# Reordered layer norm halves, masks on VectorE, GLA norm between gates, and cross attention over two sets of PSUM banks, in a streaming encoder step

## The reference

```python
x = layer_norm(ALPHA * x + 0.5 * swiglu(x, lw['w_ffn1_in'], lw['w_ffn1_out']), g[0], b[0])
mix, new_pool, ckv, kr, new_gla = token_mixing(x, pos0, pool_hist, gla_state, ckv_past, kr_past, lw)
x = layer_norm(ALPHA * x + mix, g[1], b[1])
x = layer_norm(ALPHA * x + memory_attend(x, mem_k, mem_v, lw['mem_w_q'], lw['mem_w_o']), g[2], b[2])
x = layer_norm(ALPHA * x + 0.5 * swiglu(x, lw['w_ffn2_in'], lw['w_ffn2_out']), g[3], b[3])
```

## Time and profile before

| | us |
|---|---|
| median of 3 runs | 3211.24 |
| lowest, highest | 3206.44, 3216.93 |
| profiled execution, whole | 3221.17 |
| its span in the trace | 3219.4 |

### The profile page before, as it was taken

One profiled execution on the slowest core, in us unless ns is written; L12 is line 12 of the kernel. 1 busy time (PEld: TensorE's weight loads), 2 busy tenths in 40 slices (PEclk: granted clock), 3 DMA queues, 4 the chain that ended last, 5 costly groups with the idle time before them and its releaser, 6 DMA issues.

```text
span 3219.4 us, 54799 instructions
## 1 busy us (share of the span) xinstructions
PE 3012.8 (94%) x22470; PEld 2860.8 (89%) x22470; DVE 1082.6 (34%) x1818; ACT 911.7 (28%) x1392; POOL 1092.7 (34%) x454
## 2 busy tenths in 40 slices
PE   7999999999899799999999999899998987999995
PEld 7999987689898589999999999867998975899995
DVE  3111255543335352112331112555334253511123
ACT  2222242322334232222232222432223341422223
POOL 3444322033271224434334333311333611344331
PEclk9999999999999899999999999989999998999998
DMA  3222222022252012222222222211222510222222
GB/s 134 91 85 86 92 68 68 15 73 79 75 194 66 27 53 92 88 88 86 80 83 85 91 86 79 83 40 40 67 80 88 188 53 27 71 87 85 91 87 81
DMA packets 74438, 259.83 MB, mean 81 GB/s; under 512 B 10704, under 2 KB 13648, under 8 KB 72848
## 3 DMA queue, kind: packets, MB, share of 16 engines
q1 hardware_dynamic: 65520, 238.58, 23.1%
q10 hardware_dynamic: 8736, 18.64, 1.6%
HBM read 249.32 MB, written 7.87 MB: 80 GB/s over the span
## 4 chain that ended last, share of the span: by engine, by line
PE 85%; DVE 6%; ACT 3%; issue 2%; DVEq 1%; ACTq 1%; DMA 0%; SPq 0%
PE PS L286 84%; ACT Y L836 2%; DVE XL L1193 1%; DVE Y L1193 1%; DVE CP L1713 1%; DVEq L1264 1%; ACT XH L836 1%; ACTq L1169 0%; DVE SC L1476 0%; PE PS L784 0%; PE PS L555 0%; ACT LNT L836 0%; DMA WR<-in_w 0%; DVE PT L1501 0%; DVE SC L1702 0%
## 5 line engine op out<-in xcount | busy, mean ns | idle before, releaser
L276 POOL TENSOR_TENSOR WL<-WR,WH 128x1024 fp32r<-128x1024 f32 x450 | 1092.5, 2433 | 2066.4 <-ACT WH L836 2065.8
L286 PE MATMUL PS<-XH,WH 128*128 128x272 f32 x4192 | 934.1, 294 | 54.5 <-DVE XL L1193 32.4
L286 PE MATMUL PS<-XL,WH 128*128 128x272 f32 x4192 | 923.0, 292 | 0.0
L286 PEld LDWEIGHTS PS<-XH,WH 128*128 128x128 f32 x4192 | 686.2, 191 | 73.2 <-DVE XL L1193 44.4
L286 PEld LDWEIGHTS PS<-XL,WH 128*128 128x128 f32 x4192 | 687.5, 192 | 0.1
L836 ACT ACTIVATE WH<-WR 128x1024 fp32r<-128x1024 f32 x455 | 478.6, 1056 | 690.1 <-DMA WR<-in_w 672.2
L286 PE MATMUL PS<-XH,WL 128*128 128x272 f32 x4192 | 657.4, 290 | 0.0
L286 PEld LDWEIGHTS PS<-XH,WL 128*128 128x128 f32 x4192 | 582.7, 190 | 0.0
L1193 DVE TENSOR_TENSOR LNT<-LNT,PS 128x544 f32<-128x544 f32 x88 | 63.5, 721 | 801.3 <-PE PS L286 767.5
L836 ACT ACTIVATE LNT<-PS 128x544 f32<-128x544 f32 x140 | 87.1, 623 | 770.0 <-PE PS L286 752.5
L286 PE MATMUL PS<-HL,WH 128*128 128x272 f32 x1408 | 301.4, 289 | 0.0
(11 more groups left out here) (218 smaller groups left out, 2922.2 us busy)
## 6 DMA issues: line engine op xcount, KB each, us to landing
WR<-in_w SPq DMA_DIRECT2D x455, 512.0 KB, 3.5
Y<-in_x ACTq DMA_DIRECT2D x4, 544.0 KB, 12.0
out_y<-Y ACTq DMA_DIRECT2D x1, 2176.0 KB, 6.6
MRAW<-in_mem ACTq DMA_DIRECT2D x2, 1024.0 KB, 4.9
MKs<-in_memk_in ACTq DMA_DIRECT2D x2, 1024.0 KB, 4.9
MVs<-in_memv_in ACTq DMA_DIRECT2D x2, 1024.0 KB, 8.4
out_mem_k<-MKp ACTq DMA_DIRECT2D x2, 1024.0 KB, 5.9
out_mem_v<-MVp ACTq DMA_DIRECT2D x2, 1024.0 KB, 7.9
```

The costliest lines, as they stand in the source:

```text
L276: pool.tensor_tensor(WL[s][:, :], WR[s][:, :], WH[s][:, :].bitcast(F32), ALU.subtract).then_inc(lo_ready[s], 1)
L286: return pe.matmul(out, lhsT, rhs, start=start, stop=stop, skip_group_check=True)
```

## The change

Five things, in one edit of the hand-written order:

- **Layer norm**: VectorE no longer waits for half 1 of the last group before it works on half 0: `residual_last(1)` stands after the third multiply of half 0, `head(1)` after the sixth; two subtractions run ahead instead of three. In the FFN outputs, group 7 is split by halves only from its second weight chunk on; in `wo` and `co`, groups 6 and 7 are both split. TensorE's `norm_last` for half 1 moves into the next `quad`, after chunk 3 of half 0. `quad` follows three groups chunk by chunk, and one after them. ScalarE converts one weight chunk more ahead of the norm (`hi_to(c0 + 24)`, that is the next phase's chunk 2) and two within it.
- **Masks**: the mask matmuls of MLA go (4 per head, 8 heads, 2 layers: 64 calls, each two instructions in the trace); VectorE writes -2^100 into the hidden places of PSUM in three memsets per head before the maxima.
- **MLA's opening**: queries 0 and keys 0 come first (banks 0-1, 2-3), V's projection after them, in the shadow of their reading; scores(0) before its last two groups. ScalarE copies four of V's groups, VectorE two.
- **GLA**: ScalarE copies the state increments to SBUF (`DS`), so that TensorE goes on; VectorE updates the states after round 0's mixing. Gates 2 and 3 stand between `o_ms` and `gla(0)`; each later `gla` follows two groups behind its gate.
- **Cross attention**: head h works in banks 3e to 3e+2, as in MLA, and queries 4 to 7 all use banks 6-7. Scores of two heads are issued first, and parts of `co` fill the last two heads.

The core of the diff:

```diff
-                for i in (0, 1):
+                for i in (0, 1, 2):
                     begin(i)
                 for h in (0, 1):
                     for c in range(KC):
                         pe.wait_ge(S["x_ready"], 16 * n + 8 * h + c + 1)
-                        for i in (0, 1):
+                        for i in (0, 1, 2):
                             one(i, h, c, w_used[(j0 + i) % SLOTS] if h and c == KC - 1 else None)
-                    for i in (2, 3):
-                        if h == 0:
-                            begin(i)
-                        for c in range(KC):
-                            one(i, h, c, w_used[(j0 + i) % SLOTS] if h and c == KC - 1 else None)
-
-            def ffn_in(l, name, n):
-                quad(l, name, n, XH, XL)
+                        if between is not None and h == 0 and c == 3:
+                            between()
+                    if h == 0:
+                        begin(3)
+                    for c in range(KC):
+                        one(3, h, c, w_used[(j0 + 3) % SLOTS] if h and c == KC - 1 else None)
...
+            def norm_last(l, i, h):
...
+                for g, m in enumerate(SPLIT[i]):
+                    pe.wait_ge(S["y_last"], split(l, i, h, g))
+                    r = mm(PS[:, 4 + 2 * h, 0:TH], ONES, Yf[:, ch(m, h)], False, m == KC - 1)
+                r.then_inc(S["st_s"], 1)
...
+            def second_half(l, i, parts):
+
+                for g, (j, tiles) in enumerate(parts):
+                    if g == 0:
+                        part(l, j, of(1, tiles[:2]))
+                        norm_last(l, i, 0)
+                        tiles = tiles[2:]
                     part(l, j, of(1, tiles), w_used[j % SLOTS])
...
-                        mm(PS[:, 3 * e + bank, o:o + n], q[:, i * 128:(i + 1) * 128], kt[:, 0:n], True, False)
-                        mm(PS[:, 3 * e + bank, o + n - 64:o + n], MASKED, ONES[0:1, 0:64], False, True)
+                        mm(PS[:, 3 * e + bank, o:o + n], q[:, i * 128:(i + 1) * 128], kt[:, 0:n], True, True)
...
+                pe.wait_ge(S["lat_ready"], l + 1)
                 queries(0)
                 keys(0)
+                pe.wait_ge(S["pool_lo"], l * 2 + 2)
+                for t in range(4):
+                    up(t, 4 + t)
+                scores(0)
+                up(4, 3)
+                pe.wait_ge(S["v_a"], l * 4 + 1)
+                up(5, 4)
                 queries(1)
-                scores(0)
-                queries(2)
                 for h in range(8):
                     if h < 7:
                         scores(h + 1)
+                    if h == 0:
+                        queries(2)
                     transposes(h)
...
-                        pe.wait_ge(S["sb_ok"], l + 1)
+                        pe.wait_ge(S["ds_rd"], l + 1)
...
                 m.then_inc(S["o_mm"], 1)
                 pe.wait_ge(S["ml_rd"], (l + 1) * KC)
-                gemm(l, cg + 1, [(k, *rest) for k, (t, *rest) in enumerate(gate(1))])
+                gate(1)
                 pe.wait_ge(S["o_sq"], l + 1)
                 for g in (0, 1):
                     for h in (0, 1):
                         m = mm(PS[:, 4 + 2 * g + h, 0:TH], BLK, LN_[:, g * T + h * TH:g * T + (h + 1) * TH], True, True)
                 m.then_inc(S["o_ms"], 1)
+                gate(2)
+                gate(3)
                 pe.wait_ge(S["o_lo"], l + 1)
-                for m_ in range(KC):
-                    if m_ >= 2:
-                        pe.wait_ge(*freed(l, m_ % 2, "cg", m_ // 2))
-                        span(l, "cg", gate(m_) + gla(m_))
-                    else:
-                        span(l, "cg", gla(m_))
+                gla(0)
+                gla(1)
+                for m_ in range(4, KC):
+                    gate(m_)
+                    gla(m_ - 2)
+                gla(6)
+                gla(7)
...
+                pe.wait_ge(S["cmem_in"], (l + 1) * 32)
+                scores(0)
+                scores(1)
+                queries(4)
+                transposes(0)
+                queries(5)
+                values(0)
+                transposes(1)
+                queries(6)
+                scores(2)
+                values(1)
+                queries(7)
+                transposes(2)
+                scores(3)
+                values(2)
+                pe.wait_ge(*freed(l, 3, "co", 0))
+                out(0, range(0, 4))
+                transposes(3)
+                out(0, range(4, 6))
+                values(3)
+                out(1, range(0, 6))
+                out(0, range(6, 8))
+                out(1, range(6, 8))
...
-                    square_last(n, 0)
+                    square_last(j, 0)
                     rstd(0)
-                    chunk(0, 0)
-                    square_last(n, 1)
-                    for c in range(1, 4):
+                    for c in range(KC):
                         chunk(0, c)
-                    hi_to(c0 + 2)
-                    for c in (4, 5):
-                        chunk(0, c)
+                        if c == 2:
+                            square_last(j, 1)
+                        if c == 3:
+                            hi_to(c0 + 3)
                     rstd(1)
-                    hi_to(c0 + 3)
-                    for c in (6, 7):
-                        chunk(0, c)
-                    for c in range(8):
+                    for c in range(KC):
                         chunk(1, c)
-                        if c == 2:
+                        if c == 0:
                             hi_to(c0 + 4)
...
+                    if j:
+                        act.wait_ge(S["ml_rd"], n)
+                    f(two(LNT[1] if j else O[:, 0:T]), banks2(2), ACT.Tanh, scale=0.5).then_inc(S["tb_ok"], 1)
                     if j == 0:
+                        act.wait_ge(S["ds_mm"], l + 1)
+                        f(DS[:, 0:1024].rearrange("p (b t) -> p b t", b=2), PS[:, 4:6, :], ACT.Copy)
+                        f(DS[:, 1024:1280], PS[:, 6, 0:256], ACT.Copy).then_inc(S["ds_rd"], 1)
+                    if j == 1:
                         act.wait_ge(S["sb_ok"], l + 1)
-                    else:
-                        act.wait_ge(S["ml_rd"], n)
-                    f(two(LNT[1]), banks2(2), ACT.Tanh, scale=0.5).then_inc(S["tb_ok"], 1)
-                    if j == 0:
...
-                for c in range(3):
-                    sub(0, c)
-                residual_last(1)
                 for h in (0, 1):
-                    if h == 1:
-                        for c in range(3):
-                            sub(1, c)
+                    for c in range(2):
+                        sub(h, c)
                     ve.wait_ge(S["rstd"], 2 * n + h + 1)
                     settle(ve)
                     for c in range(KC):
-                        if c + 3 < KC:
-                            sub(h, c + 3)
+                        if c + 2 < KC:
+                            sub(h, c + 2)
                         ve.drain()
                         mul(h, c)
                         if c:
                             lo(h, c - 1)
-                        if h == 0 and c == 3:
+                        if h == 0 and c == 2:
+                            residual_last(1)
+                        if h == 0 and c == 5:
                             head(1)
...
+
+                    ve.memset(PS[0:64, 3 * e, 448:512], HIDDEN)
+                    ve.memset(PS[0:64, 3 * e + 1, 256:512].rearrange("p (b t) -> p b t", b=2)[:, :, 64:128], HIDDEN)
+                    ve.memset(PS[0:64, 3 * e + 2, 192:256], HIDDEN)
+                    ve.drain()
...
+                def states():
+
+                    ve.wait_ge(S["ds_rd"], l + 1)
...
+                maxima(0)
+                maxima(1)
+                normalize(0)
+                normalize(1)
+                queries(4)
+                turned(0)
+                queries(5)
+                out_lo(0)
+                turned(1)
+                queries(6)
+                maxima(2)
+                out_lo(1)
+                normalize(2)
+                queries(7)
+                turned(2)
+                maxima(3)
+                out_lo(2)
+                normalize(3)
+                turned(3)
+                out_lo(3)
```

531 lines of the change are left out of this document (300 added, 231 removed).

## The result

| | before | changed |
|---|---|---|
| median, us (runs) | 3211.2 (4) | 3057.8 (4) |
| lowest and highest, us | 3206.4, 3216.9 | 3055.9, 3062.5 |
| profiled execution, its span, us | 3221.2, 3219.4 | 3057.2, 3055.5 |
| ratio, 95% interval | | 0.9512, 0.9498 to 0.9527 |

The change makes the kernel 4.9% faster, 153.4 us by these medians. The forecast was 3040, with 171 us of gain. The granted clock over the whole span rose from 0.967 to 0.989, and the number of matmul records fell by 96: the masks took 128 with them, and the second halved group of `wo` and `co` brought 32 sums for the norm (48 instead of 32 with `Y`, 160 instead of 144 with `LNT`, against `CST`).

A forecast was written before the change was run, and what follows sets the result against it. TensorE, busy 94% of the span, was taken as the bound, losing time to waits, half clock and needless mask matmuls. Terms 46 + 37 + 19 + 18 + 53 - 2 = 171 us off 3211 gave 3040, range 2990 to 3107.

The forecast's parts named there:

- Layer norm: All eight layer norms: three kinds of gain, 46 us in sum, between 20 and 59.
- First term: Norms behind the FFNs: VectorE's 5.04 us wait for half 1 of the last group goes, net 2.8 us each.
- second: After a norm's last chunk one group follows instead of two, less 0.4 for a larger last chunk: gain 2.6 us.
- third: Norms behind the FFNs: GpSimd makes two `WL` instead of three during the norm, worth 2 us each.
- Masks and MLA: MLA without mask matmuls, with memsets and a new opening: 18.6 us per layer, 37 in all, bounds 18 to 46.
- Gates a and b: Round 0 of the gates: ScalarE's copy to `DS` frees TensorE, 9.7 us per layer, 19 in all, between 8 and 20.
- GLA's norm: Gates 2 and 3 cover 13.0 us, less a new 3.9 us wait at `memk`: 9.1 per layer, 18, bounds 10 to 25.
- Cross attention: Of 112 us, 34.7 are lost; less 8 of new waits, gain 26.7 us per layer, 53, bounds 36 to 65.
- Start: Start of each projection: `quad` begins with three weight chunks and may wait for a `WL`, loss 2.3 us, 0 to 4.
- the median is 9.9 lower: Gains were summed against the profiled execution's 3221.2 us; the median was taken as 9.9 us lower, 3211.
- B: Waits move: VectorE and ScalarE become the path behind each edit; gain 104 us, time 3107, chance 0.24.
- D: Slower: short waits in the touched stages keep the clock at 0.50; 3220 with 40% of them, 3265 with half; chance 0.03.

The follow-up runs named there:

- the filled wait: Changed kernel with 30 unused matmuls put on TensorE ahead of the wait for `MML` in each layer; 3056.63 us.
- the first two experiments with the order: Cross attention of the changed kernel: queries 4 copied ahead of head 1's normalization, 3058.09 us; then head 0's copy to `CPT` ahead of it too, 3049.73 us.
- the second trace of before: The kernel before the change, unedited, profiled once more; 3218.38 us, span 3216.5.
- queries 4 early: Changed kernel with VectorE copying queries 4 ahead of head 1's normalization in cross attention; 3058.09 us.
- the three moves: Changed kernel with queries 4 and `CPT` copies before head 1's normalization, `normalize(3)` before `out_lo(2)`, `MML` after m = 4 with keys over four banks; 3034.34 us.
- the kernel with the copies first: Changed kernel with VectorE copying queries 4 and head 0's `CPT` before head 1's normalization in cross attention; 3049.73 us.

## Why the prediction was right or wrong

The sign, the size and the range (2990 to 3107) held; the median is 17.8 us over the forecast. Of the signs that it named one was counted wrong: 96 matmul records fewer and not 128, since the second halved group's sums were left out. Step by step:

- **What bounds the kernel** was right: TensorE's waits and the half clock behind them. Its busy time fell by 76 us, of which the masks are at most 23 (64 calls of 0.36). The stretches at half clock, without the one at the very end, add up to 181 us before and 38 after, which can carry the rest.
- **Layer norm.** First term (the wait for half 1) and second (one group left instead of two) are both shown by undoing them, 2.8 to 3.3 and 2.6 to 2.7 us per norm. The third (one conversion less, 2 us in the norms behind the FFNs) no run undoes: behind the first FFN 7.0 - 2.8 - 2.7 = 1.5 us are left for it. In the norms after `wo` and `co` the two undone terms come to 6.0, more than the 4.6 to 4.9 that were gained, and beyond the 0.44 of one more half residual it is open what takes the difference. All eight norms gave 41.1 us where 46 were forecast. The step that failed is "2.6 after the last chunk, for each norm": at the end of layer 0 the quad starts behind TensorE's jump, 7 us after the first `XL` is ready, so TensorE is the late one there and the third group gains 0.1. The jump was in the trace of before, as an idle time that ended by "issue", and I had not read it.
- **Masks and MLA**: 37 forecast, 38.0 measured, but the closeness is in part luck. Per layer the masks with their memsets were put at 6.6 + 2.9 - 1.0 = 8.5 us, and undoing them costs 10.5 in layer 0; for the rest of the opening 10.1 were forecast and 8.5 are left. Right are the price in the loop (1.0 per head for 0.9) and of the memsets (0.11, 0.17 and 0.11 us).
- **Gates a and b**: 19.4 forecast, 16.8 measured. The waits of 5.0 us are gone entirely. The term took layer 0's low clock for both; it is one that moves by 1.5 between executions.
- **GLA's norm** was the worst: 18 forecast, 11.8 measured. The cover of 12 us is right (undoing it costs 14), and the new wait for `MML` too (3.9 forecast, 3.9 measured). The step that failed is the price of that wait: it was put at its length, but half clock follows it, 1.4 and 1.6 us against the filled wait. The other mis-sized term is the half clock behind the old wait, put at 2.8 us: up to `memk` the stage fell from 75.4 to 67.4 us in layer 0 and from 74.7 to 67.3 in layer 1, and with 10.0 of old wait gone and 3.9 of new one come, 1.9 and 1.2 are left for it.
- **Cross attention**: 53 forecast, 54.4 measured, and this too is in part luck. The new waits were 2.8 (queries 5) and 1.6 (head 3) instead of 8 in all. Against that, 112 us was the width of a window, and the stage in it took 110.0, so 2 us fewer could be won; and in layer 1 a low stretch of 1.5 us remained. That GpSimd stretches normalizations was put at 2 us of waits; the first two experiments with the order show that it decides where the waits fall.
- **Start**: a loss of 2.3 forecast, +1.7 in the first pair of traces, -0.2 against the second trace of before. No effect that can be told from chance.
- **The base.** 7 of the 17.8 us are in the terms above. The others are in the step "the median is 9.9 lower": the sum of gains was made on an execution of 3221 us, some of whose loss was chance, and laid on a median of three runs (3211) that 34 later runs put at 3215 to 3217. Against those the changed kernel gains 159 us.

What is shown by undoing it, and what is not: the two terms of the layer norm, the masks and the cover of GLA's norm were each undone by a run. The new opening of MLA (17 us in both layers), the copy to `DS` in the gates (17) and the two sets of banks in cross attention (54) were not. For these 88 of the 164 us the evidence is that their stages got shorter and their waits vanished, and several edits act together in each.

**The rivals.** B (the waits move) happened at the places it named, `MML` and VectorE's chain in cross attention, but for 16.5 us in both layers (`MML` 7.7, `LNT` 5.6, `CP` 3.2) where B took 67 off the forecast. D (the clock stays low when TensorE is fed in small steps) did not: from 438 to 741 us the clock is 1.00 throughout, with waits of 0.64 to 2.1 us, four per two heads, in MLA's loop. The sign that the forecast named for being wrong, a clock of 0.50 in the heads' loop or in the chunk by chunk starts, did show, but small: 3.4 us in the loop of layer 1 (1.7 us longer there, absent from most other traces) and 3.4 us behind the first norm. The latter costs nothing: waits of 1.1 and 1.3 us stand ahead of it in every trace with this layer norm, in three of those traces (the filled wait, queries 4 early, the three moves) the clock stays 1.00 behind them, and the stage takes 181.4 us either way.

## What to carry to other kernels

When a long wait has been covered, look at what the covering work used to cover: gates 2 and 3 hid GLA's norm and uncovered the memory's split. A single move on an engine that feeds the critical one may only exchange a wait for another; here two moves gave nothing alone (`MML` earlier, queries 4 earlier), and 23 us came once what stood behind each of them was moved as well (8 of them from the order of the copies). Price a wait with the half clock that follows it, and read idle time that ended by nothing ("issue") too: it may be a jump.

## What the runs showed of the hardware

**VectorE beside GpSimd.** In the changed kernel, by tile (minimum/median/maximum ns):

```profile
L1320 DVE TENSOR_TENSOR LNT<-LNT,PS x88: 720/720/723, 44.0 to 2889.3; 128x544 f32<-128x544 f32 x88
L1320 DVE TENSOR_TENSOR XL<-Y,XH x144: 428/441/2619, 14.0 to 3048.6; 128x272 fp32r<-128x272 f32 x144
L1865 DVE TENSOR_SCALAR CP<-CP,SC x8: 334/334/2434, 1000.3 to 2561.0; 32x256 f32<-32x256 f32 x8
```

The first reads PSUM: 84 of its 88 overlap a conversion of GpSimd in time, and none is longer than 723 ns. The other two have their operands in SBUF, and take up to a whole conversion longer. Which engine starts first decides: the 19 `XL` that began while a conversion ran took 1.43 to 2.62 us, the 125 others at most 0.45; and the 14 subtractions and multiplies `Y<-Y,LNT`, also with both operands in SBUF, during which a conversion began kept their 0.44. The Trainium skill (SBUF — State Buffer, section "SBUF: two separate sides") gives the rule: the shared port pair is held by one instruction to its end, against VectorE's operations with two SBUF inputs or in a two-port mode. `XL` is of the first kind; that the one-input `CP` is of the second is a reading that fits and that no run isolates. Order on VectorE can use it: put what reads PSUM under GpSimd's conversions, as the kernel with the copies first did.

**The clock's low stretches** cost 1.5 to 1.7 us each where TensorE sets the pace, and are of two kinds. Some stand behind a certain wait in every execution. Others turn up in stages without a wait longer than 1 us: the gates and levels take 161.9 us without one (layer 0 of the kernel with mask matmuls), and of the 24 passes in the twelve traces of changed kernels 17 take 163.4 with one, three 164.9 with two, and three 166.4 to 167.9 with three or four. They shift when the kernel ahead of them gets some us shorter. A gain under 3 us should therefore be read from the stage in the trace, not from one time.
